# A DiT layer on one core: small loads and a wait moved across stage borders, and four expert tiles moved ahead

## The chip, the core and the metric

One Trainium2 chip, and one of its cores. The program is one launch. The time is device microseconds (us); the kernel before took 2840.35 us in the median of 3 runs (2839.32 to 2850.03). TensorE is called PE here, VectorE DVE, ScalarE ACT, GpSimd POOL, SyncE SP. SP issues all DMAs of this kernel.

## The reference

One layer of depth 1 on 512 latent tokens of width 1024 with 256 context tokens, batch 1, all in fp32:

```
mod  = silu(c) @ ada_w + ada_b                 # six shifts, scales, gates
h    = rmsnorm(z, norm1_g) * (1 + scale) + shift
P    = h @ w_in                                # features of all branches
y_a  = RWKV-7 branch, two directions, 8 heads of 64, first over ctx, then over x
y_b  = mLSTM branch, two directions, 4 heads, chunked, column-major order on x
x    = x + gt1 * ((sig(ga)*(y_a @ w_branch_a) + sig(gb)*(y_b @ w_branch_b)) @ w_out)
h2   = rmsnorm(x, norm2_g) * (1 + scale2) + shift2
q    = h2 @ wq;  s = q . keys                  # 8 heads, two sides of 128 keys
top 16 of each side, top 16 of the 16 x 16 sums  -> 128 experts of 16384 per token
act  = gelu(u[idx] . h2);  f = sum (softmax(score) * act) v[idx]
out  = rmsnorm(x + gt2 * f, final_g)
```

## The kernel before

The kernel is a row of stages (`phase_...`), each a block in which every engine has its own instruction list; engines wait for each other through semaphores, and a stage ends with a barrier of all five engines. Tensors are laid out with 128 channels on the partitions and tokens along the free dimension. A product whose operands must stay exact is made of three fp32r matmuls (high x high, high x low, low x high; `product`, L85 to L87), for which ACT rounds the raw tile (`..._hi`) and POOL or DVE subtracts (`..._lo`).

The stages in order, with what touches the change:

- *Front* (`phase_front`, to 224 us). The modulation, the norm, the first projections. ACT's first instruction waits for `small_in` at 64, which is cc, ident, g1 (norm1_g) and bias (ada_b). SP issues them at L194, L195, L199 and L200; between stand the first matrix of ada_w (2 MB), xT (2 MB) and ctxT (1 MB). PE makes silu(c) into rows, multiplies the first matrix (L352), sums squares of four pairs of channel tiles (L360, L361; ACT squares a pair at L279, the third only after PE has summed the first), then multiplies the second matrix and the third, which is loaded once the first is used (L205).
- *Values* (`phase_values`, to 281 us). Values and gates of the mLSTM.
- *mLSTM* (`phase_mlstm`). SP loads select, m_mask and mlstm_g at its start (L1365 to L1367); PE waits for them before its scores, and DVE before its first instruction.
- *RWKV features* of the context and of the latent tokens (`phase_rwkv_features`, twice), each followed by a scan. Each loads wa_up (512 KB) and rw_vecs (12 KB) at its start (L557, L558), and PE and DVE wait for both first.
- *RWKV output* (`phase_rwkv_output`): loads g_up and rwo_vecs (L1044, L1045).
- *Merge*, with no part in the change.
- *Route* (`phase_route`, from about 1120 to 1416 us). For four pairs of heads, PE makes queries and scores, and DVE finds the top 16 by a long list of top-8 searches. To use PE meanwhile, this stage already works on the experts' first product: `Hidden` holds it. A U tile is 128 experts; tile n is the four-way index `t * 4 + q`. SP loads u_raw (two buffers), ACT rounds it (`split`, L1869; four buffers), POOL subtracts (`rest`, L1873), PE multiplies 24 times (`multiply`), ACT takes gelu out of one of two PSUM banks into one of two `act` buffers (`gelu`, L1889), SP stores it to DRAM (`store`, L1893). A load of tile n waits for the subtraction of tile n - 2; a gelu of tile n for the store of tile n - 2, and ACT rounds tile n + 4 after gelu n. In the loop over pairs, tiles 0 to 15 are multiplied; behind it tiles 16 to 21, then PE waits for DVE's last result (`out1`), transposes the chosen slots (L2067) and multiplies 22 and 23. POOL has one other job, `choices` (L1992), which waits for DVE and on which DVE waits.
- *Weights* (`phase_weights`, to 1900 us). Tiles 24 to 87 go on, four per loop step, beside the scatter of the router's weights: for 64 tokens at a time a block of 4 MB (`w_block`) is built and stored (L2306), eight of them. At its end SP waits until the last two have landed (L2310).
- *Experts* (`phase_experts`). SP loads the first weights, V tiles and activations, and then serves the U tiles' stores and loads; PE multiplies tiles 88 to 127 (`rounds - first_t` = 10 rounds of 4) and then 32 rounds of 4 V tiles, 24 matmuls each, which add up in ps_y. Then the last norm and the store of the output.

The tile counts hang on two constants:

```
ROUTE_T, WEIGHT_T = 6, 16
first_t = ROUTE_T + WEIGHT_T
```

Of the kernel before, what the change touches and what calls it, by code (L numbers as in the profile page):

```python
# [19 lines left out]
P = 128  # L20
# [87 lines left out]
def alloc(nc, ctx):  # L108
    def sb(name, shape, dt=F32):
        return ctx.enter_context(nc.sbuf_tensor(name, shape, dt))  # L110
    return sb
# [15 lines left out]
def phase_front(nc, a, b, h_dram):  # L127

    with ExitStack() as ctx:
# [63 lines left out]
        def _(sp):  # L193
            sp.dma_start(cc[:], a["cc"]).then_inc(small_in, 16)  # L194
            sp.dma_start(b.ident[:], a["ident"]).then_inc(small_in, 16)  # L195
            sp.dma_start(ada[0], a["ada_w"][ORDER[0]]).then_inc(ada_in[0], 16)
            sp.dma_start(xx[:], a["xT"]).then_inc(x_in, 16)
            sp.dma_start(xc, a["ctxT"]).then_inc(x_in, 16)
            sp.dma_start(g1[:], a["norm1_g"]).then_inc(small_in, 16)  # L199
            sp.dma_start(bias[:], a["ada_b"]).then_inc(small_in, 16)  # L200
# [12 lines left out]
            sp.dma_start(b.w_gates[:], a["w_gates"]).then_inc(const_in, 16)  # L213

# [22 lines left out]
            sp.wait_ge(const_in, 64)  # L237
# [291 lines left out]
def phase_rwkv_features(nc, a, b, f, T, tag):  # L529

    nch = T // C
    with ExitStack() as ctx:
        sb = alloc(nc, ctx)

        def sem(name):
            return b.semaphore(nc, name + tag)

        wa_up = sb("wa_up" + tag, [P, 2, D_RWKV])
        vecs = sb("rw_vecs" + tag, [P, 6, PAIRS])
# [7 lines left out]
        vec_in = sem("rwf_in")  # L547
# [6 lines left out]

        @block.sync
        def _(sp):
            sp.dma_start(wa_up[:], a["wa_up"]).then_inc(vec_in, 16)  # L557
            sp.dma_start(vecs[:], a["rw_vecs"]).then_inc(vec_in, 16)  # L558
# [461 lines left out]
def phase_rwkv_output(nc, a, b):  # L1020

    f = b.fX
    with ExitStack() as ctx:
# [6 lines left out]
        vecs = sb("rwo_vecs", [P, 3, PAIRS])  # L1030
# [30 lines left out]
        def _(pe):  # L1061
# [15 lines left out]
            pe.wait_ge(vec_in, 32)  # L1077
# [7 lines left out]
        def _(v):  # L1085
# [8 lines left out]
            v.wait_ge(vec_in, 32)  # L1094
# [34 lines left out]
def phase_values(nc, a, b):  # L1129
# [8 lines left out]
    with ExitStack() as ctx:  # L1138
        sb = alloc(nc, ctx)

        def sem(name):
            return b.semaphore(nc, name)
# [18 lines left out]
        v_in, small_in = sem("val_in"), sem("mlg_in")  # L1161
# [11 lines left out]
        def _(sp):  # L1173
# [3 lines left out]
            sp.dma_start(ident[:], a["ident"][0:GROWS, 0:GROWS]).then_inc(small_in, 16)  # L1177

# [127 lines left out]
def phase_mlstm(nc, a, b):  # L1306
# [16 lines left out]
    with ExitStack() as ctx:  # L1323
# [5 lines left out]
        select = sb("select", [GROWS, UNITS, P])  # L1329
        mask = sb("m_mask", [P, 2, MC])  # L1330
        ng = sb("mlstm_g", [P, MH])
# [16 lines left out]
        small_in, zeroed, spread_done, ends_mm, kept = (sem(f"ml_{n}") for n in ("in", "zero", "spread", "ends", "kept"))  # L1348
# [13 lines left out]

        @block.sync
        def _(sp):
# [13 lines left out]
        def _(pe):  # L1378
# [79 lines left out]
            pe.wait_ge(small_in, 48)  # L1458
# [64 lines left out]
        def _(v):  # L1523
            link = Count(v, dve)
            v.wait_ge(small_in, 48)
# [315 lines left out]
class Hidden:  # L1841
# [7 lines left out]
    def __init__(self, nc, ctx, a, b, a_dram):  # L1849
# [7 lines left out]
        self.stored = [nc.alloc_semaphore(f"hd_stored{k}") for k in range(2)]  # L1857
        self.hi, self.lo, self.mm, self.out = (nc.alloc_semaphore(f"hd_{n}") for n in ("hi", "lo", "mm", "out"))
# [41 lines left out]
ROUTE_T, WEIGHT_T = 6, 16  # L1900

def phase_route(nc, a, b, hidden):


    with ExitStack() as ctx:
# [91 lines left out]
        def _(g):  # L1997
# [27 lines left out]
            hidden.rest(g, 5, 0)  # L2025
            hidden.rest(g, 5, 1)
            choices(PH // 2 - 1)
            for q in range(2, 6):
                hidden.rest(g, 5 + q // 4, q % 4)
            for q in range(2, 4):  # L2030
                hidden.rest(g, 6, q)

        @block.tensor
        def _(pe):
# [26 lines left out]
            for q in range(6):  # L2061
                hidden.multiply(pe, PH // 2 + q // 4, q % 4)
# [7 lines left out]
            hidden.multiply(pe, 5, 2)  # L2070
            hidden.multiply(pe, 5, 3)
# [175 lines left out]
def phase_weights(nc, a, b, hidden, w_dram):  # L2247
# [6 lines left out]
    with ExitStack() as ctx:  # L2254
# [17 lines left out]
        stored = [sem(f"w_stored{k}") for k in range(2)]  # L2272
# [19 lines left out]
        def _(sp):  # L2292
# [16 lines left out]
            for half in range(2):  # L2309
                sp.wait_ge(stored[half], 16 * (n_outer + 1))  # L2310
# [96 lines left out]
def phase_experts(nc, a, b, hidden, w_dram, out):  # L2407
# [8 lines left out]
    with ExitStack() as ctx:  # L2416
# [25 lines left out]
        def _(sp):  # L2442
# [147 lines left out]
def build_program(nc, a, out):  # L2590
    with ExitStack() as ctx:
# [24 lines left out]
        with mixers:  # L2616
            sm = alloc(nc, mixers)
            b.fX = sm("fX", [P, RW_TILES, TX])
            b.fC = sm("fC", [P, RW_TILES, TC])
            with ExitStack() as ml:  # L2620
# [7 lines left out]
                with ExitStack() as norm:  # L2628
                    b.h = alloc(nc, norm)("h_f32", [P, KT, TX + TC])
                    b.w_gates = alloc(nc, norm)("win_gates", [P, KT, F_ROW + GROWS])  # L2630
                    with ExitStack() as parts:
                        sp_ = alloc(nc, parts)
                        b.hh, b.hl = sp_("h_hi", [P, KT, TX + TC], F32R), sp_("h_lo", [P, KT, TX + TC], F32R)
                        phase_front(nc, a, b, h_dram)
                    phase_values(nc, a, b)
# [122 lines left out]
```

## Time and profile before

| | us |
|---|---|
| median of 3 runs | 2840.35 |
| the profiled execution | 2841.56 |
| its span | 2839.3 |
| PE busy | 2548.7 |
| DVE busy | 1327.9 |
| ACT busy | 1026.1 |
| POOL busy | 767.5 |

The granted clock of PE was 0.948 of full in the mean. The span is from the first to the last instruction; the rest of the execution's time lies around it. Durations of matmuls are modelled and overlap, so that a matmul that is listed with 0.39 us is followed by the next after 0.23 us; what a tile takes is read from the distance of starts. Idle time stands in square brackets behind a row, with what ended it.

### The profile page before, as it was taken

How to read it: one execution, taken by the hardware profiler on the slowest of the kernel's cores; microseconds unless marked ns; L12 is line 12 of the kernel's file. 1: busy time of each engine (PE TensorE's matmuls, PEld its weight loads, DVE VectorE, ACT ScalarE, POOL GpSimd, SP SyncE). 2: the span in 40 equal slices, each digit the busy share in tenths (PEclk: the TensorE clock that was granted, in tenths of full speed). 3: DMA queues.
4: the chain of work that ended last, by engine and by line, in shares of the span. 5: the costliest groups of instructions: out<-in, count | busy, mean ns of one | idle time of the engine just before them, and what ended most of it. 6: DMA issues, size and time to landing. Idle time of an engine off the chain costs nothing. (4 is left out here: it accounts for less than half of the span.)

```text
span 2839.3 us, 53307 instructions
## 1 busy us (share of the span) xinstructions
PE 2548.7 (90%) x19772; PEld 2098.7 (74%) x19772; DVE 1327.9 (47%) x2679; ACT 1026.1 (36%) x1763; POOL 767.5 (27%) x627
## 2 busy tenths in 40 slices
PE   5998839759995997899599999979999999999998
PEld 2884429559983875788488888868888888888886
DVE  4764345465554232499744444420014444444443
ACT  3322433423333222332266666642223222222222
POOL 1520013124422342554455555524420000000000
PEclk9999759979997998999799999989999999999999
DMA  5551000000003221422335444554436555555551
GB/s 226 184 170 37 1 8 1 9 2 0 0 5 111 88 97 33 160 92 82 107 141 184 167 169 182 214 200 145 144 118 234 188 198 187 201 184 203 182 204 60
DMA packets 164052, 349.10 MB, mean 123 GB/s; under 512 B 13512, under 2 KB 79560, under 8 KB 161936
## 3 DMA queue, kind: packets, MB, share of 16 engines
q1 hardware_dynamic: 163984, 348.19, 35.2%
q8 instruction: 44, 0.72, 0.1%
q14 instruction: 24, 0.20, 0.0%
HBM read 276.84 MB, written 71.30 MB: 123 GB/s over the span
## 5 line engine op out<-in xcount | busy, mean ns | idle before, releaser
L85 PE MATMUL ps_a<-h_hi,u_hi 128*128 128x512 f32 x1024 | 407.3, 398 | 23.5 <-PEq L105 16.5
L2537 DVE TENSOR_TENSOR v_lo<-v_raw,v_hi 128x1024 fp32r<-128x1024 f32 x128 | 158.2, 1236 | 564.9 <-ACT v_hi L2495 564.9
L86 PE MATMUL ps_a<-h_hi,u_lo 128*128 128x512 f32 x1024 | 401.1, 392 | 0.0
L87 PE MATMUL ps_a<-h_lo,u_hi 128*128 128x512 f32 x1024 | 400.9, 391 | 0.0
L2495 ACT ACTIVATE v_hi<-v_raw 128x1024 fp32r<-128x1024 f32 x128 | 135.8, 1061 | 477.7 <-PE ps_a L87 469.3
L85 PE MATMUL ps_y<-gated_hi,v_hi 128*128 128x512 f32 x768 | 299.5, 390 | 3.1 <-DVE gated_lo L2539 3.1
L86 PE MATMUL ps_y<-gated_hi,v_lo 128*128 128x512 f32 x768 | 299.5, 390 | 0.0
L87 PE MATMUL ps_y<-gated_lo,v_hi 128*128 128x512 f32 x768 | 299.3, 390 | 0.0
L85 PEld LDWEIGHTS ps_a<-h_hi,u_hi 128*128 128x128 f32 x1024 | 194.3, 190 | 62.6 <-issue 23.1
L87 PEld LDWEIGHTS ps_a<-h_lo,u_hi 128*128 128x128 f32 x1024 | 193.6, 189 | 40.8
L1889 ACT ACTIVATE act<-ps_a 128x512 f32<-128x512 f32 x128 | 76.4, 597 | 407.6 <-PE ps_a L87 407.6
L86 PEld LDWEIGHTS ps_a<-h_hi,u_lo 128*128 128x128 f32 x1024 | 194.0, 189 | 38.0
L2349 POOL TENSOR_SCALAR mixed<-iota,w_token 128x128 f32<-128x128 f32 x128 | 149.5, 1168 | 213.3 <-PE ps_w L2368 197.8
L1873 POOL TENSOR_TENSOR u_lo<-u_raw,u_hi 128x1024 fp32r<-128x1024 f32 x64 | 154.8, 2422 | 188.7 <-ACT u_hi L1869 188.7
L1873 DVE TENSOR_TENSOR u_lo<-u_raw,u_hi 128x1024 fp32r<-128x1024 f32 x64 | 78.4, 1225 | 242.4 <-ACT u_hi L1869 242.4
L85 PEld LDWEIGHTS ps_y<-gated_hi,v_hi 128*128 128x128 f32 x768 | 144.5, 188 | 33.6 <-DVE v_lo L2537 3.5
L86 PEld LDWEIGHTS ps_y<-gated_hi,v_lo 128*128 128x128 f32 x768 | 144.6, 188 | 30.1
L87 PEld LDWEIGHTS ps_y<-gated_lo,v_hi 128*128 128x128 f32 x768 | 144.5, 188 | 30.1
L1869 ACT ACTIVATE u_hi<-u_raw 128x1024 fp32r<-128x1024 f32 x128 | 134.4, 1051 | 57.4 <-DMA u_raw<-in_uT 57.4
L2400 ACT ACTIVATE w_block<-ps_w 128x512 f32 x128 | 141.2, 1103 | 0.0
L1681 POOL TENSOR_TENSOR mg_w_lo<-mg_raw,mg_w_hi 128x1024 fp32r<-128x1024 f32 x36 | 87.7, 2437 | 196.7 <-ACT mg_w_hi L1730 196.7
L2368 PEld LDWEIGHTS ps_w<-mixed 128*128 128x128 f32 x1024 | 124.1, 191 | 5.0
(497 smaller groups left out, 5314.9 us busy)
## 6 DMA issues: line engine op xcount, KB each, us to landing
u_raw<-in_uT SPq DMA_DIRECT2D x128, 512.0 KB, 3.5
v_raw<-in_v SPq DMA_DIRECT2D x128, 512.0 KB, 4.9
a_scratch<-act SPq DMA_DIRECT2D x128, 256.0 KB, 2.2
w_scratch<-w_block SPq DMA_DIRECT2D x8, 4096.0 KB, 12.0
w_ring<-w_scratch SPq DMA_DIRECT2D x64, 512.0 KB, 4.5
gated<-a_scratch SPq DMA_DIRECT2D x128, 256.0 KB, 4.9
mg_raw<-in_w_merge SPq DMA_DIRECT2D x36, 512.0 KB, 3.4
vM<-in_ada_rows SPq DMA_DIRECT2D x32, 512.0 KB, 4.7
```

Of the source, the lines that this page charges most:

```text
L85: pe.matmul(out, wh, xh, start=first, stop=False)
L86: pe.matmul(out, wl, xh, start=False, stop=False)
L87: return pe.matmul(out, wh, xl, start=False, stop=last)
L1681: g.tensor_tensor(wl[:, k], raw[:, k], wh[:, k], ALU.subtract).then_inc(w_lo, 1)
L1869: act.activation(self.uh[:, q], self.raw[:, q % 2], ACT.Copy).then_inc(self.hi, 1)
L1873: eng.tensor_tensor(self.ul[:, q], self.raw[:, q % 2], self.uh[:, q], ALU.subtract).then_inc(self.lo, 1)
L1889: act.activation(self.act[:, q % 2], self.ps[q % 2][:], ACT.Gelu).then_inc(self.out, 1)
L2349: g_.tensor_scalar(oi[:, s, SUB - 1], iota, cur[:, s, 0:1], cur[:, s, 1:2], ALU.is_equal, ALU.mult).then_inc(built_p, 1)
L2368: m = pe.matmul(ps[s][:, k, :], oi[:, s, k], oj[:, s, k], start=True, stop=True)
L2400: act.activation(wb[:, half, :, bass.ds(g * BODY + dt, SUB)].rearrange("p j t -> p t j"), ps[s][:], ACT.Copy).then_inc(evac[s], 1)
L2495: act.activation(vh[:, q], v_raw[:, q], ACT.Copy).then_inc(v_hi, 1)
L2537: v.tensor_tensor(vl[:, q], v_raw[:, q], vh[:, q], ALU.subtract).then_inc(v_lo, 1)
```

## The change

Five edits. In the front, g1 and ada_b are issued third and fourth, ahead of the first matrix and of xT and ctxT. The tensors wa_up, rw_vecs and rwo_vecs become buffers of the whole first half, loaded once in the front behind the other constants; the two feature stages and the output stage don't load or await them any more. The constants of the mLSTM stage get space on the other side of SBUF and are loaded in the values stage, whose SP waits for them at its end. The last stores of w_block are awaited by SP in the experts stage, ahead of its first load of the weights. And ROUTE_T goes from 6 to 7: tiles 22 to 25 are multiplied ahead of the transposes as well and 26 and 27 behind, POOL subtracts up to tile 25 ahead of its last `choices`, the weights stage works on tiles 28 to 91 and the experts stage on 92 to 127, in 9 rounds.

```diff
@@ phase_front, sync
             sp.dma_start(cc[:], a["cc"]).then_inc(small_in, 16)
             sp.dma_start(b.ident[:], a["ident"]).then_inc(small_in, 16)
+            sp.dma_start(g1[:], a["norm1_g"]).then_inc(small_in, 16)
+            sp.dma_start(bias[:], a["ada_b"]).then_inc(small_in, 16)
             sp.dma_start(ada[0], a["ada_w"][ORDER[0]]).then_inc(ada_in[0], 16)
             sp.dma_start(xx[:], a["xT"]).then_inc(x_in, 16)
             sp.dma_start(xc, a["ctxT"]).then_inc(x_in, 16)
-            sp.dma_start(g1[:], a["norm1_g"]).then_inc(small_in, 16)
-            sp.dma_start(bias[:], a["ada_b"]).then_inc(small_in, 16)
...
             sp.dma_start(b.w_gates[:], a["w_gates"]).then_inc(const_in, 16)
+            sp.dma_start(b.wa_up[:], a["wa_up"]).then_inc(const_in, 16)
+            sp.dma_start(b.rw_vecs[:], a["rw_vecs"]).then_inc(const_in, 16)
+            sp.dma_start(b.rwo_vecs[:], a["rwo_vecs"]).then_inc(const_in, 16)
...
-            sp.wait_ge(const_in, 64)
+            sp.wait_ge(const_in, 112)
@@ phase_rwkv_features
-        @block.sync
-        def _(sp):
-            sp.dma_start(wa_up[:], a["wa_up"]).then_inc(vec_in, 16)
-            sp.dma_start(vecs[:], a["rw_vecs"]).then_inc(vec_in, 16)
...
-            pe.wait_ge(vec_in, 32)
...
-            v.wait_ge(vec_in, 32)
@@ phase_rwkv_output
-            sp.dma_start(vecs[:], a["rwo_vecs"]).then_inc(vec_in, 16)
...
-            pe.wait_ge(vec_in, 32)
+            pe.wait_ge(vec_in, 16)
...
-            v.wait_ge(vec_in, 32)
@@ phase_values, sync
+            sp.dma_start(b.select[:], a["select"]).then_inc(next_in, 16)
+            sp.dma_start(b.m_mask[:], a["m_mask"]).then_inc(next_in, 16)
+            sp.dma_start(b.mlstm_g[:], a["mlstm_g"]).then_inc(next_in, 16)
+            sp.wait_ge(next_in, 48)
@@ phase_mlstm
-            sp.dma_start(select[:], a["select"]).then_inc(small_in, 16)
-            sp.dma_start(mask[:], a["m_mask"]).then_inc(small_in, 16)
-            sp.dma_start(ng[:], a["mlstm_g"]).then_inc(small_in, 16)
...
-            pe.wait_ge(small_in, 48)
...
-            v.wait_ge(small_in, 48)
@@ phase_route
-ROUTE_T, WEIGHT_T = 6, 16
+ROUTE_T, WEIGHT_T = 7, 16
...
-            hidden.rest(g, 5, 0)
-            hidden.rest(g, 5, 1)
+            for n in range(4 * 5, 4 * ROUTE_T - 2):
+                hidden.rest(g, n // 4, n % 4)
             choices(PH // 2 - 1)
-            for q in range(2, 6):
-                hidden.rest(g, 5 + q // 4, q % 4)
-            for q in range(2, 4):
-                hidden.rest(g, 6, q)
+            for n in range(4 * ROUTE_T - 2, 4 * (ROUTE_T + 1)):
+                hidden.rest(g, n // 4, n % 4)
...
-            for q in range(6):
-                hidden.multiply(pe, PH // 2 + q // 4, q % 4)
+            for n in range(2 * PH, 4 * ROUTE_T - 2):
+                hidden.multiply(pe, n // 4, n % 4)
...
-            hidden.multiply(pe, 5, 2)
-            hidden.multiply(pe, 5, 3)
+            hidden.multiply(pe, ROUTE_T - 1, 2)
+            hidden.multiply(pe, ROUTE_T - 1, 3)
@@ phase_weights, sync
             bodies(sp, body, after)
-            for half in range(2):
-                sp.wait_ge(stored[half], 16 * (n_outer + 1))
@@ phase_experts, sync
             sp.dma_start(fg[:], a["final_g"]).then_inc(small_in, 16)
+            for half in range(2):
+                sp.wait_ge(hidden.w_stored[half], 16 * (W_BLOCKS // 2 + 1))
```

## Rows read from the trace of the kernel before

**Rows 1.** Busy time in windows; columns per engine, PE clock, DMA share, GB/s.

```profile
25.00:32.10 7.10, 7.10 (x19) 1.33 (x17) 2.96 (x3) 0.00 (x0) 0.00 (x0) 1.00 0.01 3
...
1373.00:1397.00 24.00, 0.00 (x0) 0.00 (x0) 23.70 (x49) 0.00 (x0) 13.16 (x4) 0.55 0.06 16
1397.00:1412.00 15.00, 14.89 (x60) 12.41 (x60) 4.36 (x9) 7.53 (x9) 7.15 (x3) 0.81 0.62 190
...
1906.00:2119.00 213.00, 213.00 (x941) 176.38 (x940) 11.16 (x12) 63.29 (x83) 86.16 (x36) 1.00 0.42 145
```

**Rows 2.** Timeline of PE, experts stage: first U tile, first ps_y matmul. Start, duration.

```profile
1900.68 0.77 PE L85 MATMUL ps_a<-h_hi,u_hi 128*128 128x512 f32 x1 [16.54 <-PEq L105]
...
2120.22 0.39 PE L85 MATMUL ps_y<-gated_hi,v_hi 128*128 128x512 f32 x1
```

**Rows 3.** Timeline of the front, and DMA issues (KB, us to landing) to 60 us.

```profile
4.87 0.46 SPq L200 DMA_DIRECT2D ada_bias<-in_ada_b  x1
...
18.31 0.22 ACT L263 ACTIVATE cc_th<-cc 128x16 f32<-128x16 f32 x1 [15.51 <-DMA ada_bias<-in_ada_b]
...
25.09 7.03 PE L352 MATMUL ps_row<-fX,silu_c 128*2 128x512 f32 x16
...
33.64 1.06 ACT L279 ACTIVATE vM<-mixed 128x1024 f32<-128x1024 f32 x1 [12.19 <-PE ps_pc L361]
...
39.22 7.03 PE L352 MATMUL ps_row<-h_f,silu_c 128*2 128x512 f32 x16
...
fX<-in_ada_w SPq DMA_DIRECT2D x2, 2048.0 KB, 7.9
...
h_f<-in_ada_w SPq DMA_DIRECT2D x1, 2048.0 KB, 18.1
...
fC<-in_ctxT SPq DMA_DIRECT2D x1, 1024.0 KB, 14.6
```

**Rows 4.** Timeline at the borders into the mLSTM and the two feature stages.

```profile
280.95 0.63 PE L1381 MATMUL ps_ms<-ident,qC 128*128 128x128 f32 x4 [0.94 <-PEq L1138]
...
284.10 0.30 DVE L1529 TENSOR_TENSOR ml_spread<-gate_ends,select 36x24 f32<-36x24 f32 x2 [16.87 <-DMA mlstm_g<-in_mlstm_g]
...
374.94 0.33 SPq L557 DMA_DIRECT2D wa_up_c<-in_wa_up  x1
...
378.51 0.17 DVE L609 TENSOR_SCALAR rw_half_c<-rw_vecs_c 128x16 f32<-128x16 f32 x1 [4.83 <-DMA rw_vecs_c<-in_rw_vecs]
...
536.52 0.33 SPq L557 DMA_DIRECT2D wa_up_x<-in_wa_up  x1
...
540.15 0.17 DVE L609 TENSOR_SCALAR rw_half_x<-rw_vecs_x 128x16 f32<-128x16 f32 x1 [3.90 <-DMA rw_vecs_x<-in_rw_vecs]
```

**Rows 5.** Timeline of the route: PE's transposes, POOL, DVE's candidate sums, ACT.

```profile
1190.58 2.39 POOL L1873 TENSOR_TENSOR u_lo<-u_raw,u_hi 128x1024 fp32r<-128x1024 f32 x1 [3.04 <-ACT u_hi L1869]
...
1191.86 2.40 DVE L2161 TENSOR_TENSOR cand<-top 128x256 f32<-128x256 f32 x4
...
1362.63 1.05 ACT L1869 ACTIVATE u_hi<-u_raw 128x1024 fp32r<-128x1024 f32 x1
...
1363.42 1.42 DVE L2161 TENSOR_TENSOR cand<-top 128x256 f32<-128x256 f32 x4
...
1383.11 7.57 POOL L1992 TENSOR_TENSOR pick<-pick,top_ix_f 128x1024 f32<-128x1024 f32 x2 [24.66 <-DVE pick L2202]
...
1397.11 1.97 PE L2067 MATMUL ps_q<-ident,slot_src 128*128 128x128 f32 x8 [24.13 <-DVE slot_src L2223]
```

**Rows 6.** Border into the experts: SP's timeline, its waits, gelus, the first store's landing.

```profile
1886.88 0.33 SPq L2306 DMA_DIRECT2D w_scratch<-w_block  x1
...
SPq L2310 <- DMA w_scratch<-w_block: 11.4, 1, 11.4
...
L1889 ACT ACTIVATE act<-ps_a x39: 598/598/600, 1908.3 to 2115.0; 128x512 f32<-128x512 f32 x39
...
DMA to landing us min/median/max: 7.3/7.3/7.3
```

More of the change, by code:

```diff
@@ L105, in clear_semaphores, with alloc @@
         nc.all_engine_barrier()
-def alloc(nc, ctx):
+def alloc(nc, ctx, side="left"):
     def sb(name, shape, dt=F32):
-        return ctx.enter_context(nc.sbuf_tensor(name, shape, dt))
+        return ctx.enter_context(nc.sbuf_tensor(name, shape, dt, side=side))
     return sb
@@ L536, in sem @@
             return b.semaphore(nc, name + tag)
-        wa_up = sb("wa_up" + tag, [P, 2, D_RWKV])
-        vecs = sb("rw_vecs" + tag, [P, 6, PAIRS])
+        wa_up, vecs = b.wa_up, b.rw_vecs
         half = sb("rw_half" + tag, [P, 4, PAIRS])
@@ L546, in phase_rwkv_features @@
         ps = [ctx.enter_context(nc.psum_tensor(f"ps_rf{k}" + tag, [P, 512], F32)) for k in range(4)]
-        vec_in = sem("rwf_in")
         tanh_wd, half_done, proj = sem("rwf_tanh"), sem("rwf_half"), sem("rwf_proj")
@@ L1029, in phase_rwkv_output @@
         g_up = sb("g_up", [P, D_RWKV])
-        vecs = sb("rwo_vecs", [P, 3, PAIRS])
+        vecs = b.rwo_vecs
         sq = sb("rwo_sq", [P, 2, PAIRS, TX])
@@ L1160, in phase_values @@
         ps_t = [ctx.enter_context(nc.psum_tensor(f"ps_gt{k}", [P, 512], F32)) for k in range(2)]
-        v_in, small_in = sem("val_in"), sem("mlg_in")
+        v_in, small_in, next_in = sem("val_in"), sem("mlg_in"), sem("mls_in")
         v_mm, v_out, g_mm = sem("val_mm"), sem("val_out"), sem("val_g_mm")
@@ L1327, in sem @@
             return b.semaphore(nc, name)
-        select = sb("select", [GROWS, UNITS, P])
-        mask = sb("m_mask", [P, 2, MC])
-        ng = sb("mlstm_g", [P, MH])
+        select, mask, ng = b.select, b.m_mask, b.mlstm_g
         spread = sb("ml_spread", [GROWS, 2, n_c + n_x, per])
@@ L1347, in phase_mlstm @@
         ps_i = [ctx.enter_context(nc.psum_tensor(f"ps_mi{k}", [P, 512], F32)) for k in range(2)]
-        small_in, zeroed, spread_done, ends_mm, kept = (sem(f"ml_{n}") for n in ("in", "zero", "spread", "ends", "kept"))
+        zeroed, spread_done, ends_mm, kept = (sem(f"ml_{n}") for n in ("zero", "spread", "ends", "kept"))
         kc_mm, kc_done, kx_mm, kx_done = sem("ml_kc_mm"), sem("ml_kc"), sem("ml_kx_mm"), sem("ml_kx")
@@ L1361, in cols @@
             return b.g_cols[:, kind // 2, chunks, kind % 2, 32 * z + heads.start:32 * z + heads.stop]
-        @block.sync
-        def _(sp):
-            sp.dma_start(select[:], a["select"]).then_inc(small_in, 16)
-            sp.dma_start(mask[:], a["m_mask"]).then_inc(small_in, 16)
-            sp.dma_start(ng[:], a["mlstm_g"]).then_inc(small_in, 16)
         @block.gpsimd
@@ L1857, in __init__ @@
         self.stored = [nc.alloc_semaphore(f"hd_stored{k}") for k in range(2)]
+        self.w_stored = [nc.alloc_semaphore(f"w_stored{k}") for k in range(2)]
         self.hi, self.lo, self.mm, self.out = (nc.alloc_semaphore(f"hd_{n}") for n in ("hi", "lo", "mm", "out"))
@@ L2271, in phase_weights @@
         built_p, fetched, turn = sem("w_built_pool"), sem("w_fetched"), sem("w_turn")
-        stored = [sem(f"w_stored{k}") for k in range(2)]
+        stored = hidden.w_stored
         block = ctx.enter_context(nc.Block())
@@ L2619, in build_program @@
             b.fC = sm("fC", [P, RW_TILES, TC])
+            b.wa_up = sm("wa_up", [P, 2, D_RWKV])
+            b.rw_vecs = sm("rw_vecs", [P, 6, PAIRS])
+            b.rwo_vecs = sm("rwo_vecs", [P, 3, PAIRS])
             with ExitStack() as ml:
@@ L2634, in build_program @@
                         phase_front(nc, a, b, h_dram)
+                    later = alloc(nc, ml, "right")
+                    b.select = later("select", [GROWS, UNITS, P])
+                    b.m_mask = later("m_mask", [P, 2, MC])
+                    b.mlstm_g = later("mlstm_g", [P, MH])
                     phase_values(nc, a, b)
```

## The prediction

> **What bounds the kernel now.** I read the page first: part 2 has PE at 90% or more of nearly every slice, with dips at the stage borders, and part 4's chain that ended last is PE all through the last third. Then the busy time in windows. The experts stage has PE busy 213.0 of 213 us at full clock [rows 1]: there every PE instruction counts. Its forty U tiles (24 matmuls each) start at 1900.68 and the first ps_y matmul starts at 2120.22 [rows 2]; less 1.9 us for a start at half clock, that is (219.5 - 1.9)/40 = 5.44 us a tile. The route's tail is the opposite: PE 0.00 busy of 24 us before 1397, DVE 23.70 busy, clock 0.55 [rows 1]. Third, who waits for whom at each border [rows 3 to 6]: a stage begins with an all-engine barrier, so what is loaded or awaited there is on everybody's path.
>
> **The change, part by part.**
>
> *Front, g1 and ada_b ahead of the large loads.* ACT's first tanh starts at 18.31, released by ada_bias, and the first row product on PE follows at 25.09, 6.8 us later [rows 3]. The bias is issued at 4.87 behind 5 MB. Ahead of them it is issued near 3.5; other small vectors land 2 to 3 us after issue when nothing large is ahead (the 12 KB rw_vecs, issued right behind wa_up's 374.94, is used at 378.51 [rows 4]), so tanh at about 6, the product at 12.8, its end at 19.8. Its matrix is issued at 3.9 and takes 8 us, 11.9, in time. But ACT's squares need xT and ctxT, and ctxT lands 14.6 us after issue at 3.4 [rows 3], at 18.0, and now 1.4 us later (two issues ahead) at 19.4. From there: the first two pairs squared by 22.5, first pair summed so that ACT can start the third at 23.5 (before: 33.64). From the third pair to the second product took 39.22 - 33.64 = 5.6 us [rows 3], so that starts at 29.1 and not 39.22. Its matrix landed at 5.4 + 18.1 = 23.5 [rows 3], now about 25. The third matrix is issued when the first product ends, at 19.8, behind 6.5 us of loads, and lands near 33, before it is wanted at 36. Gain **10.1 us**; the rest of the stage follows DVE and then PE and only shifts. Bounds 6 (a matrix late) to 12.
>
> *mLSTM constants loaded in the values stage.* PE starts the stage at 280.95, DVE at 284.10, released by the constants' DMA [rows 4]. With them there, DVE does the two spreads at once, but its next step needs PE's four transposes, done at 281.6: it starts there and not at 284.4. **2.8 us** (bounds 2.5 and 3.2). The loads go behind wv in a stage of 56 us; SP's new wait is over long before its end.
>
> *wa_up and rw_vecs loaded once in front.* Both feature stages start with two DMAs at 374.94 and 536.52, and DVE waits for them to 378.51 and 540.15 [rows 4]. DVE is the chain there (kk, then ACT's square, then everything else), so **3.5 + 3.6 us**. Three more issues (0.5 MB) in the front lie behind other constants where DMA idles. rwo_vecs gains nothing: its stage still waits for g_up, and neither of the two ends a wait there.
>
> *Four more U tiles behind the route.* They leave the experts stage: 4 x 5.44 = **21.8 us** off a stretch in which PE never idles. In the route they need 4 x 5.44 = 21.8 us of PE, and 24 us are idle [rows 1]: last of them done at 1394.8, the transposes released at 1397.11 by DVE [rows 5]. So they fit by 2.3 us. Their feed: ACT splits tile 23 at 1362.63 [rows 5], POOL's subtraction takes 2.4 us, the next load is issued when the tile two before is subtracted and comes back in about 4.5; that is 8.3 us for two tiles, faster than PE. On POOL the last `choices` now stands behind six subtractions and not two. The sixth (tile 25) needs tile 21 multiplied and evicted at 1373 and is over at 1377; `choices` is released by DVE at 1383.11 [rows 5], so it isn't late, with 6 us to spare. After it everything is as before with tile numbers four higher. Two effects on the end of the route. PE doesn't idle 24 us ahead of the transposes; after that idle it ran them and nine matmuls at the slower clock (mean 0.81 over 15 us [rows 1]), against which I set +2.6 us of gain. And POOL's earlier subtractions run beside DVE's chain. The row: DVE's four candidate sums (L2161) take 1.42 us alone and 2.40, from 1191.86, when POOL subtracts from 1190.58 to 1192.97 [rows 5]. Tile 23's subtraction now starts at 1363.7, in the middle of the same four sums at 1363.42 [rows 5], so I take -2.0 us (bounds 0, and -4.8, two subtractions in full). The other DVE work in that stretch is top-8 searches, with the same durations under POOL work as without. Net for the route **0.6 us** (-3 to +2.6).
>
> The Trainium skill has a rule that speaks against this part ("SBUF — State Buffer", Who interferes with whom): a DVE instruction with two SBUF inputs and a GpSimd instruction that reads SBUF exclude each other, and the second to issue blocks until the first ends. By that rule the three remaining sums wait for the whole subtraction, which an estimate puts at 2.4 us; the 2.40 us group agrees with it.
>
> *The last store of w_block waited for in the experts stage.* SP waited 11.4 us for it at the end of the weights stage [rows 6], and every engine with it: PE idles 16.54 us before 1900.68 [rows 2], and SP issues the store at 1886.88 [rows 6], as ACT ends its last build. Take the wait away and next late are these two, both over by 1887.2; the barriers cost 1.9 us as before. **11.4 us**, PE starts at 1889.2. What is queued behind the wait on SP: fg is not, but the first loads of w, v and a, then the stores of the U tiles and the loads of the tiles after. Four U tiles are split and subtracted and two more are in raw, so PE runs four (to 1913) without SP. Tile 2's eviction needs tile 0's store, though: act has two buffers. SP passes at 1898.8 and issues ten loads (4 MB); tile 0's store goes behind them at about 1906. In the trace of before the same store, issued at 1909.1 after the gelu of 1908.3 and behind the same ten loads, took 7.3 us to land [rows 6], to 1916.4; the loads now start 1.8 us earlier, so about 1914.6, against 1912.9 when PE wants that bank. A stall of 0 to 2.5 us; I take **-1.3**. After it PE takes 5.44 us a tile and the feed 5, so nothing more comes. Net 10.1.
>
> On that store the Trainium skill ("DMA: Bandwidth & Descriptors", Queues, rings and completion order) says that each DMA engine takes its descriptors in ring order. By it the store can't land before the ten loads have moved; the 7.3 us agree.
>
> **Sum.** 10.1 + 2.8 + 3.5 + 3.6 + 0.6 + 10.1 + 21.8 = 52.5 us off the profiled execution's 2841.56 (span 2839.3 and 2.3 around it): 2789.1. That execution is 1.2 us over the median of 2840.35, so **2788 us**.
>
> **Rivals.**
>
> (a) *The front gains little.* If the squares or a matrix come later than I have them (the sum rests on xT and ctxT landing by 19.4), or PE, now with two pauses of about 2 us between its first products, runs them at half clock, then 4 us is left of 10: 2794. For it: the loads are the only thing that moves there by bytes and not by order. Against: DMA idles from 25 to 32 in the trace of before [rows 1].
>
> (b) *The route's end moves out.* DVE 4.8 us later through POOL, and PE idle long enough before the transposes to fall to half clock (2.5 us): 2794 to 2796. For it: the 2.40 us row. Against: only one group of sums meets a subtraction by my times.
>
> (c) *The wait at the experts' border only changes place.* PE stalls behind the store for all that it ran ahead, say 6 of the 11.4 us: 2793. For it: two act buffers and the 7.3 us. Against: four tiles are 22 us of work and SP is back after 10.
>
> (d) *Slower than before.* The U feed never recovers in the experts stage: loads and stores of U stand behind one another on SP, two tiles per 16.6 us in place of 10.9, PE pauses in each tile and drops to half clock. At 2.9 us a tile more, all 36 tiles lose 104 us: 2892; it decides from 19 tiles on (19 x 2.9 = 55). Against it: ACT's evictions in the trace of before come every 5.4 us right behind the same ten loads (39 of them from 1908.3 to 2115.0 [rows 6]).
>
> (e) *Better than summed.* With the border idle of PE down from 16.6 to 5 us and the front's pauses short, the clock stays up and the store isn't late: another 5 us, 2783.
>
> **How the numbers follow.** Forecast 0.62, (a) 0.10, (b) 0.10, (c) 0.08, (d) 0.02, (e) 0.08. The bounds of the unknown costs are -4, +2 in the front, -3.6, +2 in the route, -4, +1.3 at the experts' border; not all at one end, they make about 2779 to 2797. With (a) to (c) at the upper side, 2776 to 2800 holds 8 in 10. A measurement here tells 0.5%, 14 us, from no change; only (d), or most of the gains failing together, ends within it or over it: faster 0.97, same 0.02, slower 0.01.
>
> **What would show it.** In the profile of the changed kernel: tanh near 6 us and the second row product near 29; no wait for mlstm_g, rw_vecs_c and rw_vecs_x; between the last U tile and the ps_q transposes PE idles 2 to 5 us and not 24; one L2161 group longer by 2 us; PE's pause before the experts stage 5 us and not 16.5, and perhaps one of 1 to 2 us five tiles on; 36 U tiles ahead of the first ps_y matmul, some 196 us. If the w_block store still holds all engines, or the U tiles in the route push the transposes out, the prediction is wrong.

## The result and the profile after

The changed kernel took 2799.1 us in the median of 4 executions, beside 2843.36 for the kernel before in 4 of the same chip: a ratio of 0.9861, 95% interval [0.9832, 0.989], some 40 us less (the two medians themselves lie 44.3 us apart). The forecast was 2788 with a range of 2776 to 2800; by the ratio the time is 2801 (0.9861 x 2840.35), just above the range. Faster as forecast, but by 40 us where 52 were summed. The four times are 2820.51, 2801.11, 2797.08 and 2789.43, in the order of their granted clocks: 0.940, 0.950, 0.951 and 0.955. The execution that was profiled is the slowest of them (span 2818.5 us).

Its front, ACT first and then PE (start, duration, engine, line, operation, tiles; in brackets the idle time before and what ended it). ACT's line is the tanh, then the third pair of squares; PE's are the first and the second row product:

```profile
4.79 0.22 ACT L266 ACTIVATE cc_th<-cc 128x16 f32<-128x16 f32 x1 [1.99 <-DMA ada_bias<-in_ada_b]
...
23.43 1.06 ACT L282 ACTIVATE vM<-mixed 128x1024 f32<-128x1024 f32 x1 [1.61 <-PE ps_pc L364]
```

```profile
11.41 7.03 PE L355 MATMUL ps_row<-fX,silu_c 128*2 128x512 f32 x16 [0.46 <-DMA fX<-in_ada_w]
...
30.10 7.03 PE L355 MATMUL ps_row<-h_f,silu_c 128*2 128x512 f32 x16
```

The third pair starts at 23.43 (forecast 23.5, before 33.64) and the second product at 30.10 (forecast 29.1, before 39.22) [rows 3]. PE at the later borders, and DVE at the start of the features:

```profile
273.00 0.63 PE L1369 MATMUL ps_ms<-ident,qC 128*128 128x128 f32 x4 [0.94 <-PEq L1130]
...
275.13 2.07 PE L1385 MATMUL ps_ms<-qX 64*128 64x128 f32 x8 [1.28 <-DVE ml_kw_c L1522]
...
1408.60 1.97 PE L2052 MATMUL ps_q<-ident,slot_src 128*128 128x128 f32 x8 [4.83 <-DVE slot_src L2208]
...
1898.64 0.77 PE L85 MATMUL ps_a<-h_hi,u_hi 128*128 128x512 f32 x1 [4.97 <-PEq L105]
...
1925.32 0.47 PE L85 MATMUL ps_a<-h_hi,u_hi 128*128 128x512 f32 x1 [2.48 <-ACT act L1876]
...
2099.50 0.39 PE L85 MATMUL ps_y<-gated_hi,v_hi 128*128 128x512 f32 x1
```

```profile
391.70 0.17 DVE L603 TENSOR_SCALAR rw_half_c<-rw_vecs 128x16 f32<-128x16 f32 x1 [1.30 <-PEq L105]
```

All waits that were to go are gone: PE idles 4.83 us before the transposes and not 24.13 [rows 5], 4.97 before the experts stage and not 16.54 [rows 2], and no constant is waited for in the mLSTM and feature stages [rows 4]. But compare the distances. From PE's start in the mLSTM stage to DVE's start in the features it is 391.70 - 273.00 = 118.7 us; before it was 378.51 - 280.95 = 97.6 [rows 4]. The forecast had it 6.3 us shorter. So 27.4 us went there. The busy time in windows shows why (columns: busy time of PE, of PE's weight loads, of DVE, ACT and POOL, then PE's granted clock, DMA share, GB/s); first the kernel before, then the changed one:

```profile
272.00:320.00 48.00, 42.83 (x185) 21.08 (x185) 15.47 (x35) 12.82 (x42) 0.53 (x1) 0.93 0.02 7
320.00:366.00 46.00, 24.89 (x144) 16.61 (x142) 16.42 (x53) 25.88 (x92) 4.39 (x4) 0.62 0.00 1
```

```profile
272.00:320.00 48.00, 45.78 (x108) 19.27 (x108) 11.68 (x25) 8.58 (x29) 0.53 (x1) 0.53 0.00 0
320.00:366.00 46.00, 42.25 (x198) 27.96 (x196) 15.66 (x51) 18.33 (x68) 0.00 (x0) 0.50 0.00 1
```

PE's clock went to its lower level (1.2 GHz, shown as 0.50) at 275 us, in the 1.28 us pause ahead of the scores, and stayed there for the whole stage, with PE busy 88.0 of 94 us. PE does the same work in nearly twice the time: the scores of two heads, 2.07 us here, take 1.16 at the upper level. In the kernel before the clock was low from 283.2 to 290.1 us and again from 331 us on, in the changed one from 275 us to the end of the stage, so the loss arises ahead of 331.

### The profile page after: what moved, and what is told of

The parts are those of the page before. It is cut to its first block and busy times, and to the rows that moved or that the text cites. A ratio compares the mean times of both kernels' runs of the same rounds, so it can differ in the third digit from the quotient of the medians.

```text
span 2818.5 us, 53257 instructions
## 1 busy us (share of the span) xinstructions
PE 2583.1 (92%) x19772; PEld 2115.8 (75%) x19772; DVE 1331.7 (47%) x2679; ACT 1026.9 (36%) x1763; POOL 768.5 (27%) x627
## 5 line engine op out<-in xcount | busy, mean ns | idle before, releaser
L2332 POOL TENSOR_SCALAR mixed<-iota,w_token 128x128 f32<-128x128 f32 x128 | 149.5, 1168 | 213.3 <-PE ps_w L2351 197.7
```

The lines of the kernel that those rows point to most:

```text
L2332: g_.tensor_scalar(oi[:, s, SUB - 1], iota, cur[:, s, 0:1], cur[:, s, 1:2], ALU.is_equal, ALU.mult).then_inc(built_p, 1)
```

## The experiments

Theory: the five edits brought what was summed, to within some 5 us, and this execution lost 27 us, others less, because the clock level of the mLSTM stage differs between executions. Rivals: the loss lies elsewhere and the clock is a by-product; or single edits brought less than summed. Four groups of kernels were run, each group on one chip with the kernel before beside it (medians of before: 2848.7, 2849.1, 2840.6 and 2846.3).

**The changed kernel once more.**

> The changed kernel once more, unaltered, to see what varies. Theory (clock): the edits gave what was forecast, about 50 us, and the profiled execution lost 27.6 us of it in the mLSTM stage, where the granted clock was 0.50 from 275 us to the stage's end; executions differ in whether that stage is at full clock. Then its times lie between 2788 and 2821, and in a profile with the mLSTM stage at full clock the span is about 2790; with it at 0.50 it is 2815 to 2820. Rival (the loss is elsewhere): the times lie close together near 2800 whatever that stage's clock is.

Measured: 2804.43 us (2791.41 to 2816.14, 6 executions). The profiled one took 2793.28, and its windows are:

```profile
272.00:320.00 48.00, 42.50 (x233) 22.59 (x233) 21.15 (x57) 18.58 (x67) 0.53 (x1) 0.96 0.00 1
320.00:366.00 46.00, 21.71 (x96) 14.33 (x96) 19.07 (x46) 23.11 (x71) 5.43 (x4) 0.50 0.00 1
```

The same instructions, the same pause of 1.28 us: here the clock fell at 275.4 and was back at 278.8, after 3.4 us, and from PE's first mLSTM matmul to the features it took 362.90 - 272.41 = 90.5 us. That is 28.2 us less in this stage, where the two executions differ by 27.2 in all, so the rest is as good as equal. Only one execution of each kernel was profiled; of the others the mean granted clock is on record, and over all 16 executions of the changed kernel the time falls as it rises, from 2821 us at 0.94 to some 2790 at 0.955. The kernel before isn't steady either: its 11 executions beside this run took 2837 to 2868 us.

**The pause made longer.** One edit undone:

```diff
@@ phase_values, sync
-            sp.dma_start(b.select[:], a["select"]).then_inc(next_in, 16)
...
@@ phase_mlstm
+            sp.dma_start(select[:], a["select"]).then_inc(small_in, 16)
...
+            pe.wait_ge(small_in, 48)
```

> The changed kernel with one part undone: select, m_mask and mlstm_g are loaded at the start of the mLSTM stage again, so PE pauses some 3 us before its second group there. Theory (clock level set by how the stage begins): with the pause back the stage starts at half clock, rises after some 7 us as in the kernel before, and is at 1.00 from about 283 to 320; median 2795 to 2800 and the times within some 10 us of each other. Rival (chance): the stage's clock varies between executions as much as in the changed kernel, and the median is 2.8 us over that kernel's. Rival (sum as forecast, clock of no account): 2.8 us over.

Measured: 2802.5 us (2793.58 to 2807.55). No guess holds as written. PE's pause was 3.02 us again, and the clock, low from 272.6, came back only at 303.3 and not after some 7 us as in the kernel before, so how the stage begins doesn't fix how long the clock stays low. The times lie within 14 us and not 10, and the median is 1.9 us under that of the changed kernel and not 2.8 over it: the edit's 2.8 us are lost in the scatter here.

**The pause filled.** Two matmuls that nobody reads, into a bank that is free:

```diff
             mm.then_inc(ends_mm, 1)
+            for k in range(2):
+                pe.matmul(ps_i[k % 2][:], b.ident[:], b.qX[:, 0, :], start=True, stop=True)
 
             def scores(h):
```

> The changed kernel with two more fp32 matmuls (ident x qX, 128x512, about 1 us each) on PE in the mLSTM stage, into a bank that isn't used yet, just where PE waits 1.28 us for DVE. Theory: it was that wait, right behind the barrier's 0.94 us, that lowered the clock; filled, the clock stays at 1.00 to about 325 and the time is 2788 to 2792 in every execution, though PE does 0.8 us more. Rival: the barrier alone lowers it, or the stage's own matmuls do; then the clock is 0.50 in this stage in some executions still and the median is that of the changed kernel.

Measured: 2791.81 us (2787.64 to 2794.08, 6 executions), ratio to before 0.9803 [0.9768, 0.9839]. Its start of the stage, and the windows (of PE, the other engines, clock):

```profile
272.57 0.30 PE L1373 MATMUL ps_me<-ml_spread,ones 36*64 36x24 f32 x4
272.80 1.98 PE L1377 MATMUL ps_mi<-qX,ident 128*128 128x512 f32 x4
274.72 1.16 PE L1387 MATMUL ps_ms<-qX 64*128 64x128 f32 x8
```

```profile
272.00:320.00 48.00, 44.10 (x244) 23.46 (x244) 21.93 (x59) 19.11 (x68) 0.50 (x1) 0.99 0.00 1
```

The pause is gone, 1.98 us of work standing where 1.28 us of idleness stood, and the clock stays up, to 319 us.

> The same with eight such matmuls, 8 us at full clock: more than the wait. Theory: if the clock has fallen, these wide matmuls of all 128 rows raise it, since those of the same form did so in the values stage; then the stage's scores run at 1.00 and the median is about 2788 + 7 = 2795 with little spread. Rival (no matmul in this stage raises it): 0.50 through the stage, 2820 + 15 = 2835.

Eight of them: 2793.69 us (2790.81 to 2796.84), and 1.00 through the window. The extra six cost 2 us and not 5. In the profiles this stage is 6.1 us longer than with two (95.2 against 89.1 from PE's first matmul to the features) and the stretch behind it, up to the latent features, 3.8 us shorter; why it is shorter isn't explained.

**Each edit by itself,** taken out of the kernel with the two fill matmuls, since that one scatters over 6 us and not 25 to 32. That base is fill2, measured on the first chip; the kernels here ran on others, and each scatters over 8 to 10 us, so their sizes hold to a few us. The kernel before had nearly the same median beside three of them (2849.1 against 2848.7), and its lowest time was 2836.9 to 2837.1 on all three chips. First the border into the experts:

```diff
@@ phase_weights, sync
+            for half in range(2):
+                sp.wait_ge(stored[half], 16 * (n_outer + 1))
@@ phase_experts, sync
-            for half in range(2):
-                sp.wait_ge(hidden.w_stored[half], 16 * (W_BLOCKS // 2 + 1))
```

> From here on the base is the changed kernel with two matmuls in the mLSTM pause (median 2791.8), since its times spread less. Here SP waits for the last stores of w_block in the weights stage again. In the traces that edit brought 11.6 us at the border and gave back 3.2 us in two places between U tiles (36 tiles in 200.9 us and not 197.7). Theory: 8.4 us slower than the base, 2800; PE idle about 16.5 us before its first U tile and in no place behind. Rival (the wait only changes place, case c of the prediction): 5 us or less slower, 2797 or below.

Measured: 2798.8 us, 7.0 over the base; PE waits for the store again:

```profile
1879.79 0.77 PE L85 MATMUL ps_a<-h_hi,u_hi 128*128 128x512 f32 x1 [16.67 <-PEq L105]
```

and no gap follows up to the first ps_y matmul at 2077.26, 197.5 us later. Between the two profiles the stretch before this matmul is 11.8 us longer and the one behind it 3.3 us shorter than in the base, 8.5 us in all, as expected; the median has 7.0.

> The base with g1 and ada_b behind ctxT again. Theory: the front's order brought 7.5 to 9.3 us up to the values stage in the two traces, so 8.5 us slower than the base, 2800. Rival (a of the prediction, half clock between the products takes it back): 4 us or less, 2796.

Measured (two lines moved back behind ctxT): 2801.96 us, 10.2 over the base.

> The base with ROUTE_T at 6. Theory: the four U tiles cost 21.8 us in the experts stage; in the route they cost 2.3 us (DVE's four sums took 3.7 us and not 1.42 beside POOL's subtractions) and gave 1.2 us back by the clock. So 21.8 - 1.1 = 20.7 us slower than the base, 2812.5. Rival (b of the prediction, the route's end moves out by 5 to 7 us): 15 us slower, 2807.

Measured (`ROUTE_T, WEIGHT_T = 6, 16`): 2812.42 us, 20.6 over the base; PE idles 24.19 us before the transposes again.

> The base (changed kernel with two fill matmuls) with wa_up and rw_vecs loaded and awaited in both feature stages again. Theory: 3.5 + 3.6 us slower, 2799. Rival (PE or ACT is late there anyway): under 3 us.

Measured (both DMAs and both waits back in the feature stages): 2798.93 us, 7.1 us over the base. The kernel before had a median 8 us lower in this group, but the same lowest time, so fewer of its executions lay high there and nothing is to be added to the 7. The profiles agree: 4.5 us more from PE's start in the mLSTM stage to the features, and 3.0 more from there to the latent features.

**The stall behind the first store.** What the forecast set at 1.3 us is 2.48 in the profile above, and the U stretch takes 2099.50 - 1898.64 = 200.9 us where 36 tiles make 36 x 5.44 + 1.9 = 197.7, so 3.2 in all. By the starts of its matmuls PE loses 2.65 us at this one pause; most of the rest lies at the start, where the clock was low for 4.6 us here and 3.9 before. No second pause follows. SP and ACT of the changed kernel there:

```profile
1896.40 0.33 SPq L2291 DMA_DIRECT2D w_scratch<-w_block  x1
...
1908.21 0.41 SPq L2430 DMA_DIRECT2D w_ring<-w_scratch  x1
...
1916.31 0.35 SPq L1880 DMA_DIRECT2D a_scratch<-act  x1
```

```profile
1924.57 0.60 ACT L1876 ACTIVATE act<-ps_a 128x512 f32<-128x512 f32 x1 [11.04 <-DMA a_scratch<-act]
```

The store of tile 0, issued behind ten loads, took 8.2 us to land. So the ten were spread:

```diff
@@ phase_experts, sync
-            for half in range(2):
-                sp.wait_ge(hidden.w_stored[half], 16 * (W_BLOCKS // 2 + 1))
             for q in range(G):
-                if q % 2 == 0:
-                    load_w(0, q // 2)
+                hidden.store(sp, first_t, q)
+                hidden.next_load(sp, first_t, q)
                 load_va(0, q)
+            for q in range(G):
+                hidden.store(sp, first_t + 1, q)
+                hidden.next_load(sp, first_t + 1, q)
+                if q < 2:
+                    sp.wait_ge(hidden.w_stored[q], 16 * (W_BLOCKS // 2 + 1))
+                else:
+                    load_w(0, q - 2)
-            with sp.Fori(0, rounds - first_t - 2) as i:
+            with sp.Fori(2, rounds - first_t - 2) as i:
```

> The base with the first loads of the experts stage spread over its first eight U tiles: a v_raw and a gated load behind each of the first four tiles' stores, the waits for w_block's stores and the two w_ring loads behind the next four. Theory: the stall behind tile 0's store (2.5 us of 3.2) is that store standing behind ten loads; spread, it lands in some 2 to 3 us, PE never waits, 3 us faster than the base, 2788.6. Rival (the store is slow for other reasons, or the U loads come late): same as the base, 2791.8, with a pause elsewhere.

Measured: 2788.63 us (2784.5 to 2790.47), 3.2 under the base. That store now lands in 2.0 us:

```profile
DMA to landing us min/median/max: 2.0/2.0/2.0
```

and the first ps_y matmul comes 2068.18 - 1870.07 = 198.1 us after the first U tile, 2.6 us less than in the base (200.7). The Trainium skill ("DMA: Bandwidth & Descriptors", Queues, rings and completion order) has each DMA engine take its descriptors in ring order. The two traces agree: 8.2 us behind ten loads, 2.0 us without them.

**POOL beside DVE's sums.** DVE and POOL of the changed kernel in the route's tail:

```profile
1369.01 1.42 DVE L2146 TENSOR_TENSOR cand<-top 128x256 f32<-128x256 f32 x4
1372.44 3.73 DVE L2146 TENSOR_TENSOR cand<-top 128x256 f32<-128x256 f32 x4
```

```profile
1369.79 2.90 POOL L1860 TENSOR_TENSOR u_lo<-u_raw,u_hi 128x1024 fp32r<-128x1024 f32 x1 [2.43 <-ACT u_hi L1856]
1372.94 2.62 POOL L1860 TENSOR_TENSOR u_lo<-u_raw,u_hi 128x1024 fp32r<-128x1024 f32 x1 [0.24 <-ACT u_hi L1856]
```

The second group of sums is 2.3 us longer (forecast 2.0), and POOL's two subtractions are 0.5 and 0.2 us longer than their 2.40. One wait keeps them apart:

```diff
@@ phase_route, gpsimd
             for n in range(4 * 5, 4 * ROUTE_T - 2):
+                if n == 4 * 5 + 2:
+                    dve_s.wait(g, PH // 2 - 1, "cand1")
                 hidden.rest(g, n // 4, n % 4)
```

> f_spread (2788.6) with one more wait: POOL doesn't subtract U tile 22 before DVE has its last candidate sums. Theory: POOL's subtractions of tiles 22 and 23 are what made those four sums 3.73 us long instead of 1.42; then they take 1.42 again, the transposes come 2.3 us earlier, and the time is 2786.3; tile 22 is subtracted some 4 us later, well ahead of PE, which idles 4.8 us before the transposes. Rival (another load on DVE, or the feed of tile 25 now ends last): 2788.6 or more.

Measured, DVE and then PE:

```profile
1342.19 1.43 DVE L2150 TENSOR_TENSOR cand<-top 128x256 f32<-128x256 f32 x4
```

```profile
1376.04 1.10 PE L2056 MATMUL ps_q<-ident,slot_src 128*128 128x128 f32 x8 [2.60 <-DVE slot_src L2212]
```

The sums take 1.43 us, POOL's subtractions 2.4 us again, PE idles 2.60 us, and the transposes run at the upper level (1.10 us for eight, where 1.97 stood). The median, 2788.24 us, is about that of f_spread on another chip (2788.63) and doesn't show the gain. The profiles do: from the latent features to the weights stage it takes 878.0 us here and 881.9 in f_spread, 3.9 us less, where 2.3 by the sums and 1.5 by the clock were expected.

**The kernel before with the pause filled.**

> The kernel before with the same kind of fill at the start of its mLSTM stage: three matmuls where PE waits 2.9 us for the stage's constants, one where it waits for DVE. Theory (the clock of this stage spreads the times of both kernels, 2837 to 2868 here): the stage stays at 1.00 and the median is 2838 to 2840, the times within 8 us. Then the five edits are worth 2839 - 2791.8 = 47 us at equal clocks. Rival (the kernel before spreads for another reason): median 2846 to 2849, spread over 20 us.

Measured: 2838.15 us (2832.09 to 2841.75, 12 executions), ratio 0.9983 [0.9969, 0.9997]. The scatter shrinks from 18.6 us to 9.7, but on this chip the kernel before lies at 2840.62 by itself, so the fill is worth 2.5 us there and not 9. The clock was at 1.00 in its profile from the start of the stage to 329 us. The lowest time of the kernel before on this chip, 2836.89, lies between the lowest and the highest with the fill. With both pauses filled the five edits are worth 2838.2 - 2791.8 = 46 us, across chips.

**Filling further on.** One more matmul behind every second of the last 13 units:

```diff
             for n in range(first_x, last):
                 unit(n)
+                if n >= first_x + 3 and (n - first_x) % 2 == 1:
+                    pe.matmul(ps_s[0][:], b.ident[:], b.qX[:, 0, :], start=True, stop=True)
```

> f_late with one more matmul of the fill's form behind every second of the last 13 units of the mLSTM stage, where the clock fell at 318 to 320 us in nearly every profile with PE busy. Theory: the clock stays at 1.00 there, a unit takes 1.75 us and not 2.52, so 5 us faster than f_late, 2781. Rival (the added work costs what it brings, or the clock falls all the same): the same as f_late or up to 6 us slower.

Measured: 2798.25 us, 10 us slower than f_late. The clock part came: 0.69 from 320 to 366 us where f_late has 0.50. But the features start only 1.0 us earlier: PE was busy 21.5 of those 46 us in f_late and so doesn't set the end of that stage. And in the scan 300 us later PE stands still twice with nothing awaited, up to 672 and up to 768 us:

```profile
672.19 4.11 PE L880 MATMUL ps_rs_x<-pr_x,qs_x 64*64 64x192 f32 x24 [4.70 <-issue]
```

```profile
768.68 1.83 PE L880 MATMUL ps_rs_x<-pr_x,qs_x 64*64 64x192 f32 x9 [4.85 <-issue]
```

Each also lowered the clock for some 7 us, and the stretch from the latent features to the weights stage is 15 us longer than in f_late. None of the other 17 profiles has such a pause. The trace names no releaser, but it has a lead, the queue that the page calls instruction (packets, MB, share), first of f_late, then of this kernel:

```profile
q8 instruction: 45, 0.74, 0.1%
```

```profile
q8 instruction: 63, 1.03, 0.2%
```

From 640 to 840 us it moves 25 packets here and 5 to 7 in every other profile. In each of the two pauses two of them moved (0.03 MB) and nothing else did, and in the 8 us ahead of each pause no queue moved anything. If that queue brings the program to the engines, this kernel fetches more of it in the scan than any other here, and PE stands still where it does. That the one causes the other is likely and not shown: no run changed these transfers alone.

**On one chip.** Four kernels: changed, changed with fill, that with the spread loads and POOL's wait, and the last without the fill.

> The changed kernel on the chip of the next three, so that they can be compared. Theory (clock of the mLSTM stage): times scattered from 2789 to 2817, median near 2802, over 10 us above the kernel with the two fill matmuls. Rival (the 12.6 us between the two medians were the chip's or chance): within 4 us of it.

> The changed kernel with the two fill matmuls again. Theory: 2792, within 4 us up and down in every execution.

> Fill, spread loads and POOL's wait together. Theory: 3.2 us less than the fill alone by the spread loads (stall behind tile 0's store), and 2.3 us less by DVE's sums at 1.43 us; its profile showed PE idle 2.6 us and no more before the transposes and full clock through them, which is 1.5 us more: 2785 to 2786. Rival (POOL's wait moves nothing at the end): 2788.6.

> The same without the two fill matmuls, so the pause in the mLSTM stage is open again. Theory: the clock of that stage is once more left to the execution: times scattered over 15 to 30 us, median 8 to 12 us above the kernel before this one, lowest time near 2785. Rival (the fill helped by something other than the clock, or only by chance): as the kernel before this one.

| kernel | median us | lowest to highest | ratio to before, 95% |
|---|---|---|---|
| changed | 2797.67 | 2789.43 to 2821.27 | 0.9837 [0.9801, 0.9873] |
| with fill | 2790.95 | 2787.08 to 2791.27 | 0.9801 [0.9779, 0.9823] |
| fill, spread, POOL's wait | 2784.09 | 2781.3 to 2786.85 | 0.9783 [0.9761, 0.9804] |
| spread, POOL's wait, no fill | 2797.16 | 2784.74 to 2812.16 | 0.9826 [0.9794, 0.9858] |

With the fill the times lie within 4 and 6 us, without it within 32 and 27, and the lowest times without it are 2.4 and 3.4 us above those with it. The profile of the changed kernel has this stage at the lower level again, from 274.7 to 343 us and from 346 on (span 2818.1). Twelve profiles of kernels with the fill have the upper level from the start of this stage to 316 us or later; of the six without it (before among them) each has it low for a while there: 3.4 us (after_again), 6.9 (before), 27 (late_only), 31 (mls_undone), 68 (same_after) and to the end of the stage (the profile above). So the rival of same_after is settled: it is the pause, and not the chip. The third kernel beats both kernels of the case, the changed one by 13.6 us on this chip. Its gain over the fill alone, 6.9 us, is near the 3.2 + 2.3 + 1.5 that were expected.

## Why the prediction missed, step by step

Two profiled executions of the changed kernel against the profile of before, by the distances between the same instructions (us gained):

| stretch, up to | summed | execution of 2820.5 us | execution of 2793.3 us |
|---|---|---|---|
| PE's first matmul of the values stage | 10.1 | 7.5 | 9.3 |
| PE's first of the mLSTM stage | 0 | 0.4 | -0.7 |
| DVE's first of the features (context) | 2.8 + 3.5 | -21.1 | 7.1 |
| DVE's first of the features (latent) | 3.6 | 6.5 | 6.8 |
| PE's first of the output stage | 0 | -1.5 | -1.3 |
| ACT's first of the weights stage | 0.6 | -1.4 | -2.8 |
| PE's first U tile of the experts stage | 11.4 | 11.6 | 11.2 |
| first ps_y matmul | 21.8 - 1.3 | 18.7 | 18.6 |
| end | 0 | 0.1 | -0.1 |
| sum | 52.5 | 20.8 | 48.1 |

The miss has two parts. With the clock up the edits are worth 46 to 48 us and not 52.5: the terms of the route and of the border were too high. The other part, 7 to 13 us of the changed kernel's median, is the clock in the mLSTM stage; the kernel before loses 2.5 us there, on the chip where it was measured. Together that is 35 to 43 us, and 39.5 was measured.

- *Front: right.* 9.3 us in the execution of 2793.3, 10.2 when taken out. Every time of the forecast's chain came within 1.4 us. Rival (a) happened in part, by the execution: in both PE idled 3.05 us before its first sums; in that of 2820.5 us the clock then fell for 3.5 us and 1.8 us of the ten went, in the other it stayed up.
- *mLSTM constants: right in place, of no worth in the median.* DVE starts with PE, and without the edit the median is not higher (2802.5 against 2804.4). What it uncovered, a stage that PE enters with a short pause, is the failed step.
- *The failed step: the term of the mLSTM stage, "2.8 us (bounds 2.5 and 3.2)".* The forecast costed each edit with the clock of the one profiled execution, set 0 without a reason for the rest of the mLSTM stage, and its list of unknown costs has bounds for the front, the route and the border and none for this stage; rival (e) even took it that shorter pauses keep the clock up. A pause of 1.28 us right behind the barrier's 0.94 was enough to lower it in all three profiles of the changed kernel, and what it then costs is 0 to 27 us, by the execution. No rival had that, so the range was too narrow above: of 16 executions of the changed kernel, nine lie over 2800, and the median of all is 2801.8.
- *Feature vectors: right.* 7.1 us when taken out, 7.1 summed. The other 3 us of the latent row in the table aren't assigned: profiles of kernels with the same instructions in this stretch have 153.6 to 157.4 us for it.
- *Four U tiles: right in kind, 2 us off.* 20.6 us when taken out, against 21.8 + 0.6 = 22.4. They fitted by 4.8 us and not 2.3. DVE lost 2.3 us (4.64 - 1.42 = 3.2 in the execution of 2793.3 us) where I had 2.0, and I had the +2.6 by the clock too high: after 4.83 us of idleness the transposes still took 1.97 us. This part of rival (b) is what happened, without its 5 us. The rule of the Trainium skill ("SBUF — State Buffer", Who interferes with whom) that spoke against the edit holds: beside two subtractions the four sums took 3.73 and 4.64 us, and kept apart, both are back at their own durations (1.43 and 2.4 us).
- *Store awaited in the experts stage: right, the stall under-sized.* PE started 11.2 to 11.6 us earlier (11.4). The loss behind it was 3.2 us and not 1.3, 2.65 of them in the stall: SP passed at 1908.2, 9.6 us after PE's start as forecast, but tile 0's store was issued 17.7 us after that start and not 16.8, and landed after 8.2 us and not 7.3. Rival (c) had 6. Taking the wait out brought 7.0 us net by the medians and 8.5 by the profiles, where 10.1 was summed.
- *Rivals (d) and (e):* PE paused once, after four tiles, and never again, so nothing of (d); its 16.6 us for two tiles stands in no row. The fastest execution with all pauses open, 2789.4, is near the forecast's 2788 and not (e)'s 2783.
- *The range.* The bounds as listed, all at one end, give 2783 to 2799.6; the lower 2779 of the text doesn't follow from them. A bound for the clock of the mLSTM stage would have moved the upper end by up to 27 us.

So the likeliest case described the execution with the clock up to 4.4 us (48.1 against 52.5), and the error was to take one state of the clock for granted.

## What to carry to other kernels

A profile is one execution: where a stage begins with PE pausing a microsecond or two behind a barrier, compute the stage at both clock levels, put the dearer one into the range, and look at the scatter of the times before trusting a sum. When a change shortens a wait to a small rest, fill the rest with idle matmuls of PE; two of them were worth 7 to 13 us here. And a wait that is moved behind a border has its price in the queue behind it: spread the loads among the stores that somebody waits for.

## What the runs showed of the hardware

- The clock can stay at the lower level through long work. The Trainium skill ("TensorE: Matmul & The Clock Gate", What's actually happening) has it that activity releases the throttle. The values stage fits that (low for 3.4 us at its start in the changed kernel, then up), the mLSTM stage doesn't: 88.0 us busy of 94 (by the modelled durations) at 0.50 to 0.53 in one execution, back at the upper level after 3.4 us in another, with the same instructions. There the measurement decides, and what else the release needs stays open. The same page (Seeing it yourself) warns that the clock's records can be unreliable; here they hold, since the starts go with them: the instruction behind the same eight matmuls starts 2.00 us after them in the one case (277.13 - 275.13) and 1.08 in the other (275.80 - 274.72).
- Matmuls that only fill a pause of 1.28 us decide over 0 to 27 us: in twelve profiles with such matmuls the clock never fell at that place.
- PE can stand still for 4.7 us with nothing awaited in a stage that wasn't edited, after matmuls were added to an earlier one (f_units). In that stretch the queue of instructions moved 25 packets and 5 to 7 in the other profiles, two of them in each pause; that they are the cause isn't shown.
